# Attention outputs computed transposed, with V stationary in high and low halves

## The reference

```python
s = einsum('bghqd,bgnd->bghqn', qb, kc) * scale
p_cmp = masked_softmax(s, cmp_end <= t)            # cmp: 63 compressed keys
o_cmp = einsum('bghqn,bgnd->bghqd', p_cmp, vc)
...                                                # slc: 16 of 16 blocks of 64 keys are taken
p = masked_softmax(s, pos <= t)
o_slc = einsum('bghqk,bgqkd->bghqd', p, v_sel)
...                                                # win: the last 512 keys
o_win = einsum('bghqk,bgkd->bghqd', p, vwb)
out = gb[..., 0:1] * o_cmp + gb[..., 1:2] * o_slc + gb[..., 2:3] * o_win
```

## Time and profile before

| | us |
|---|---|
| median of 3 runs | 1504.34 |
| lowest, highest | 1502.41, 1508.38 |
| the profiled execution | 1505.05 |
| its span, first to last instruction | 1503.2 |
| attention, four trips | 342 to 683 |

### The profile page before, as it was taken

The page is one execution under the profiler, slowest core; times in us unless marked ns, Lnnn a source line. Parts: engine busy times, 40 slices in busy tenths (PEclk is TensorE's granted clock), DMA queues, the critical chain, the costliest instruction groups (busy, mean ns, idle before and its releaser), DMA issues.

```text
span 1503.2 us, 23026 instructions
## 1 busy us (share of the span) xinstructions
PE 1443.0 (96%) x7958; PEld 1234.4 (82%) x7958; DVE 874.7 (58%) x1633; ACT 627.6 (42%) x1242; POOL 162.3 (11%) x179
## 2 busy tenths in 40 slices
PE   7999999998989899998999998999999999999999
PEld 6888888877878888888997886888888788888887
DVE  2002682106657475668876486666666588668764
ACT  5113302224544445453241256765555654444441
POOL 2433333520000000000033000000000000000000
PEclk9999999999989899899999999999999999999999
DMA  5211114200000000003010014544444865643332
GB/s 165 64 49 49 46 33 125 70 7 2 1 1 0 1 0 1 0 0 134 22 55 31 29 36 142 167 154 153 148 150 152 285 240 168 225 140 99 98 113 84
DMA packets 78248, 129.25 MB, mean 86 GB/s; under 512 B 8973, under 2 KB 26826, under 8 KB 78154
## 3 DMA queue, kind: packets, MB, share of 16 engines
q1 hardware_dynamic: 77968, 128.01, 26.9%
q10 hardware_dynamic: 186, 0.08, 0.0%
HBM read 94.51 MB, written 33.55 MB: 85 GB/s over the span
## 4 chain that ended last, share of the span: by engine, by line
PE 88%; DVE 7%; ACT 2%; issue 2%; DMA 1%; DVEq 0%; ACTq 0%
PE ps L516 62%; PE ps L2120 7%; PE ps L2080 4%; PE ps L2095 4%; PE ps L2143 3%; PE ps L2114 1%; PE ps L1949 1%; PE ps L2085 1%; PE ps L1921 1%; PE ps L2064 1%; PE ps L755 1%; DVE hgrn_A L1618 1%; DVE hgrn_vg L1652 0%; DVE hgrn_k L1609 0%; PE ps L2188 0%
## 5 line engine op out<-in xcount | busy, mean ns | idle before, releaser
L516 PE MATMUL ps<-mlp_w_high,hidden_high 128*128 128x512 f32 x448 | 174.3, 389 | 0.0
L516 PE MATMUL ps<-mlp_w_low,hidden_high 128*128 128x512 f32 x448 | 174.3, 389 | 0.0
L516 PE MATMUL ps<-mlp_w_high,hidden_low 128*128 128x512 f32 x448 | 174.3, 389 | 0.0
L516 PE MATMUL ps<-w_high,hT_high 128*128 128x512 f32 (+1 forms) x448 | 170.5, 380 | 1.6 <-DVE hT_low L1373 0.9
L516 PE MATMUL ps<-w_low,hT_high 128*128 128x512 f32 (+1 forms) x448 | 168.1, 375 | 0.0
L516 PE MATMUL ps<-w_high,hT_low 128*128 128x512 f32 (+1 forms) x448 | 168.0, 375 | 0.0
L2120 PE MATMUL ps<-nsa,probs_T 128*128 x1056 | 139.1, 276 | 0.0
L1683 DVE TENSOR_TENSOR mlp_w_low<-mlp_w_raw,mlp_w_high 128x512 fp32r<-128x512 f32 x112 | 77.1, 691 | 98.3 <-ACT mlp_w_high L1209 98.3
L1308 ACT ACTIVATE mlp_w_high<-mlp_w_raw 128x512 fp32r<-128x512 f32 x112 | 70.6, 630 | 148.3 <-PE ps L516 148.3
L2120 PEld LDWEIGHTS ps<-nsa,probs_T 128*128 128x128 f32 x1056 | 130.5, 195 | 0.0
L1763 DVE TENSOR_TENSOR mlp_w_low<-mlp_w_raw,mlp_w_high 128x512 fp32r<-128x512 f32 x112 | 77.2, 689 | 65.8 <-ACT mlp_w_high L1308 65.8
(11 more groups left out here) (232 smaller groups left out, 2922.1 us busy)
## 6 DMA issues: line engine op xcount, KB each, us to landing
hidden_raw<-hidden_pieces SPq DMA_DIRECT2D x112, 256.0 KB, 2.7
mlp_w_raw<-in_w_mlp_in_dram SPq DMA_DIRECT2D x32, 512.0 KB, 4.4
hidden_pieces<-hidden SPq DMA_DIRECT2D x64, 256.0 KB, 2.7
mlp_w_raw<-in_w_mlp_out_dram SPq DMA_DIRECT2D x64, 256.0 KB, 4.6
w_raw<-in_w_in_dram SPq DMA_DIRECT2D x56, 256.0 KB, 2.7
hidden_pieces<-hidden_s SPq DMA_DIRECT2D x48, 256.0 KB, 2.2
x_in<-in_x_dram SPq DMA_DIRECT2D x8, 512.0 KB, 6.8
w_raw<-in_w_out_dram SPq DMA_DIRECT2D x16, 256.0 KB, 2.6
```

The source lines that it names most:

```text
L516: ins = nc.tensor.matmul(out_ap, a_hl[i], b_hl[j], start=first and n == 0, stop=last and n == 2, skip_group_check=onto_a_sum_already_read)
```

## The change

V of the slc and win branches is split before the loop into a high half (fp32r) and the rest, and laid out as 64 high and 64 low columns for each kind and group (v_split, in nsa). The transposed probabilities of two token tiles t-1 and t lie side by side as 256 columns, in a high and a low half (PT, two sets): ScalarE copies every group out of its PSUM bank as the high half, then VectorE subtracts for the low half, and both must be done before TensorE writes the bank again. For each pair of token tiles TensorE holds a V block of 128 columns and streams the 256 high and then the 256 low columns (outputs_T): rows 0 to 63 of the result are from V's high half, 64 to 127 from its low one. slc and win fill one bank together. ScalarE copies the bank (oT), TensorE transposes it back in four blocks (outputs_back) into the seventh bank, ScalarE copies that to o_rows, and GpSimd adds the halves, multiplies by the coefficients and adds both branches onto nsa, four operations a pair (rows_pool). VectorE forms the coefficients once for a pair. The cmp items stay as they were, with ScalarE making their copy.

The new buffers take hv's place: SP stores hv to DRAM (hv_kept) as its quarters are ready, the last two after the masks, and loads it again after the last rows of attention (y_done), ahead of w_out; ScalarE, GpSimd and TensorE wait for the stores (TensorE through the memsets of the unused blocks, zeroed). TensorE's loop over g and both of GpSimd's loops are written out. The HGRN2 stage now begins with the last transposes back (oT_back). The w2 loads of four chunks share one semaphore and the hidden loads use x_loaded.

```diff
@@ -297,7 +291,15 @@
     KS_L = sb("k_low", [P, 2, NG, S], F32R, 16384)
     QT = sb("q_stack", [P, 2, S], F32R, 32768)
     probs = sb("probs", [P, P_SLOTS, S], F32, 65536)
-    pT = sb("probs_T", [P, PT_SLOTS, BW], F32, 40960)
+    W2T = 2 * P
+    PT = [{"slc": [sb(f"probs_T_slc{n}_{s}", [P, ns, W2T], F32R, a) for s, a in zip(("high", "low"), at2)],
+           "win": [sb(f"probs_T_win{n}_{s}", [P, 6, W2T], F32R, a) for s, a in zip(("high", "low"), at3)]}
+          for n, ns, at2, at3 in ((0, 6, (HV_AT, HV_AT + 6144), (HV_AT + 12288, HV_AT + 18432)),
+                                  (1, 8, (40960, 49152), (83968, HV_AT + 24576)))]
+    cmp_pT = sb("cmp_probs_T", [P, BW], F32, 59392)
+    oT = sb("outputs_T", [P, BW], F32, 57344)
+    o_rows = sb("outputs_high_low", [P, 4, 2, DK], F32, HV_AT + 30720)
+    v_split = sb("v_high_low", [P, NT, NSAW], F32R, NSA_AT)
     masks = sb("masks", [P, 3 * P], BF16, 61440)
     cmask = sb("cmask", [P, NT * NCP], BF16, 62464)
     cdiff = sb("cmp_diff", [P, BW], F32, 81920)
...
-        n = it.groups[m]["ptn"] - PT_SLOTS
-        if n >= 0:
-            old = [u for u in it.groups if u.get("ptn") == n][0]
-            eng.wait_ge(pv_done, ib + (old["item"] + 1))
+    def pt_slots(j, m):
+        kind, hh, t, tiles = it.items[j]
+        u = it.groups[m]
+        r = 1 - t % 2 + u["first"]
+        cols = slice(t % 2 * P, (t % 2 + 1) * P)
+        return [x[:, r:r + u["n"], cols] for x in PT[t // 2 % 2][kind]]
+    def by_head(c0, part):
+        return v_split[:, :, c0:c0 + 4 * DK].rearrange("p t (g a d) -> p t g a d", g=NG, a=2)[:, :, :, part, :]
+    def v_rows(c0):
+        return nsa[:, :, c0:c0 + 2 * DK].rearrange("p t (g d) -> p t g d", g=NG)
+    V_AT = {"slc": KC0, "win": KS0}
+    hv_kept = nc.dram_tensor("hgrn_v_and_gate", (P, 2, NT, HH * P), F32, kind="Internal").ap()
     def flat(ap):
...
                         load_chunk(sp, n, j, w_in0[j * P:(j + 1) * P, bass.ds(i * BW + col0, BW)])
+            def store_hv(i, half):
+                sp.wait_ge(proj_out, 40 + 8 * i + 4 * half + 4)
+                sp.dma_start(hv_kept[:, i, 4 * half:4 * half + 4, :], hv[:, i, 4 * half:4 * half + 4, :]).then_inc(hv_stored, 16)
+            for half in range(2):
+                store_hv(0, half)
             sp.wait_ge(w_used, W_OUT_AT)
...
+            for half in range(2):
+                store_hv(1, half)
+            sp.wait_ge(oT_back, 4 * NPT)
             sp.dma_start(tree[:, :, :].rearrange("p n t -> p (n t)"), c_tree).then_inc(t_loaded, 16)
+            sp.wait_ge(y_done, 4 * NPT + 1)
+            for i in range(2):
+                sp.dma_start(hv[:, i, :, :], hv_kept[:, i, :, :]).then_inc(hv_loaded[i], 16)
             for m in range(16):
                 if m == RING:
                     sp.wait_ge(q_up, 2)
...
+            pool.wait_ge(hv_stored, 64)
+            for n in range(2):
+                for kind, r, c0 in (("slc", 0, 0), ("win", 0, 0), ("win", 5, P)):
+                    for x in PT[n][kind]:
+                        pool.memset(x[:, r, c0:c0 + P].bitcast(F32), 0.0).then_inc(zeroed, 1)
+            pool.sem_inc(y_done)
+            ys = Steps(y_step)
+            def rows_pool(g, pr, n):
+                trip = g * 2 + pr
+                hh, t = n // 4, 2 * (n % 4)
+                u = o_rows[:, :, 0, :]
+                u4 = u.rearrange("p (b t) d -> p b t d", b=2)
+                y = nsa[:, t:t + 2, bass.ds(g * 256 + pr * 128 + hh * DK, DK)]
+                c = coef[:, hh, t:t + 2, :].rearrange("p t b -> p b t").unsqueeze(3).to_broadcast([P, 2, 2, DK])
+                pool.wait_ge(o_out, trip * NPT + (n + 2))
+                ys.mark(pool.tensor_tensor(u, u, o_rows[:, :, 1, :], ALU.add))
+                pool.wait_ge(coef_ready, trip * NPT + (n + 1))
+                ys.wait(pool)
+                ys.mark(pool.tensor_tensor(u4, u4, c, ALU.mult))
+                ys.wait(pool)
+                pool.wait_ge(cmp_y, trip * 2 + (hh + 1))
+                ys.mark(pool.tensor_tensor(y, u4[:, 0, :, :], y, ALU.add))
+                ys.wait(pool)
+                pool.tensor_tensor(y, u4[:, 1, :, :], y, ALU.add).then_inc(y_done, 1)
+            for g in range(NG):
+                for pr in range(2):
                     trip = g * 2 + pr
                     pool.wait_ge(t_full, trip * len(it.groups) + FIRST)
                     stand_alone(pool)
                     stage_head(None, 1, nsa[:, :, bass.ds(g * 256 + pr * 128 + DK, DK)])
-                    stage_head(None, 0, nsa[:, :, bass.ds(g * 256 + pr * 128 + 2 * DK, DK)])
+                    col = (trip + 1) * 2 * DK if trip < 3 else KW0
+                    stage_head(None, 0, nsa[:, :, col:col + DK])
+                    for n in range(NPT):
+                        rows_pool(g, pr, n)
             pool.wait_ge(f_up, 14)
...
                 act.wait_ge(t_full, 8 + half + 1)
                 act.activation(QT[:, 0, half * BW:(half + 1) * BW], ps[:, key_bank(8 + half), :], ACT.Copy).then_inc(t_act, 1)
+            act.activation(by_head(KC0, 0), v_rows(VS0), ACT.Copy).then_inc(v_high, 1)
+            act.wait_ge(v_low, 1)
+            act.wait_ge(stage_ready, 4)
+            act.activation(by_head(KS0, 0), v_rows(VW0), ACT.Copy).then_inc(v_high, 1)
+            act.sem_inc(o_out)
             def out_act(act, c):
                 act.wait_ge(O_full, c + 1)
...
+                def outputs_T_act(i, n):
+                    act.wait_ge(pv_done, i * NPT + (n + 1))
+                    if n:
+                        act.wait_ge(oT_back, i * NPT + n)
+                    act.activation(oT[:], ps[:, O_BANK, :], ACT.Copy).then_inc(oT_out, 1)
+                def output_rows_act(i, n):
+                    act.wait_ge(oT_back, i * NPT + (n + 1))
+                    act.wait_ge(y_done, i * NPT + (n + 1))
+                    act.activation(o_rows[:].rearrange("p i a d -> p (i a d)"), ps[:, B_BANK, :], ACT.Copy).then_inc(o_out, 1)
                 table_for(act, ACT.Exp)
                 exponentials(0)
...
+                        act.wait_ge(t_full, tb + (m + 1))
+                        n = it.pair_of(j)
+                        if kind == "cmp":
+                            if hh:
+                                act.wait_ge(cmp_pv_done, i * 2 + 1)
+                            act.activation(cmp_pT[:], ps[:, T_BANK + m % 2, :], ACT.Copy).then_inc(t_act, 1)
+                            continue
+                        if n >= 2:
...
+                            .then_inc(t_act, 1)
                     if j + 2 < len(it.items):
                         exponentials(j + 2)
+                    if it.second(j - 1) and it.items[j - 1][0] == "win":
+                        outputs_T_act(i, it.pair_of(j - 1))
+                    if it.second(j - 2) and it.items[j - 2][0] == "win":
+                        output_rows_act(i, it.pair_of(j - 2))
+                outputs_T_act(i, NPT - 1)
+                output_rows_act(i, NPT - 1)
+            act.wait_ge(hv_stored, 64)
             with act.Fori(0, NG) as g:
...
+            for n, (kind, c0) in enumerate((("slc", VS0), ("win", VW0))):
+                dve.wait_ge(v_high, n + 1)
+                dve.tensor_tensor(by_head(V_AT[kind], 1), v_rows(c0), by_head(V_AT[kind], 0).bitcast(F32), ALU.subtract).then_inc(v_low, 1)
...
-                    at_.mark(dve.reciprocal(c, rsums[:, hh, t, :]))
+                    at_.mark(dve.reciprocal(c, rsums[:, hh, t - 1:t + 1, :]))
                     at_.wait(dve)
-                    at_.mark(dve.tensor_tensor(c, c, gates[:, t, bass.ds(head3 + 1, 2)], ALU.mult))
-                    at_.wait(dve)
-                    dve.wait_ge(pv_done, ib + (j + 1))
-                    dve.wait_ge(o_free, i * 18 + (hh * 9 + 1))
-                    o_bank = O_BANK + it.pair(j) % 2
...
+                        high, low = pt_slots(j, m)
+                        dve.wait_ge(t_act, ab + u["act_after"])
+                        dve.tensor_tensor(low, ps[:, T_BANK + m % 2, 0:u["n"] * P].rearrange("p (n t) -> p n t", t=P),
+                                          high.bitcast(F32), ALU.subtract).then_inc(t_dve, 1)
+                    if kind == "win" and it.second(j):
+                        coefficients(j)
+                    if j >= 2 and it.items[j - 2][0] == "cmp":
+                        cmp_rows(j - 2)
             with dve.Fori(0, NG) as g:
                 with dve.Fori(0, 2) as pr:
...
                             pe.wait_ge(exp_done, ib + (u + 1))
                         if it.items[u][0] == "cmp":
-                            pe.wait_ge(o_free, i * 18 + (it.items[u][1] * 9 + 1))
+                            pe.wait_ge(cmp_y, i * 2 + (it.items[u][1] + 1))
                     if kind == "cmp":
                         pe.wait_ge(t_dve, vb + (it.groups[it.prep[1][1]]["dve_after"] if hh else 0))
...
                 def transposes(j):
                     pe.wait_ge(exp_done, ib + (j + 1))
```

(51 more changed lines are left out.)

167 lines of the change are left out of this document (72 added, 95 removed).

## The result

The changed kernel takes 1520.86 us (median; 1519.32 to 1525.32) against 1505.39 of the kernel before beside it: ratio 1.011, 95% interval 1.0084 to 1.0135. It is slower by some 16 us. I had said 1497, faster or the same, with 1514 as the upper end: both side and range were wrong.

The account below looks back on a forecast made before the run. TensorE, busy 79.2 of 85.7 us a trip, was taken to set the pace; -32.4 + 21 + 3.6 - 2.4 + 1.0 = -9.2 us, gain rounded down by 1, took 1505 to 1497, with 8 in 10 for 1478 to 1514.

Parts of the forecast that it names:

- Removed work: TensorE's output products in attention: old ones out, new ones and transposes back in, -46.8 + 14.4 = -32.4 us over four trips.
- Work taken from TensorE counts in full: Attention trips: TensorE sets the pace, so its savings count whole while the transposes, ScalarE, VectorE chain stays shorter.
- The bank round: Transposing banks passing through ScalarE, then VectorE: 2.13 us a round, waits of 5.2 us a trip, 21 in four (0 to 40).
- No engine's sum reaches TensorE's 70: Attention trips: VectorE near 56 us, ScalarE 61, GpSimd 2.3 a pair, all below TensorE's 70.
- rival (b): Attention pairs: ScalarE's copies fall into the bank round, 0.6 us at each of 32 pairs, +19, 1516 us; chance 13%.
- Start: Before attention's first scores: V is split first, in two rounds of about 2.25 us, +3.6 us (bounds +3.5 and +8.5).
- Rival (a): Trip tails: the clock falls, the last two outputs take twice as long, 13 us in four trips, 1510 us; chance 25%.
- (c): Bank round in attention: costs nothing, so without its 21 us the forecast is 1476 us; chance 15%.
- (d): Start of attention: held by the store to DRAM, +5 us on the forecast, 1502 us; chance 5%.
- Boundaries: Between trips: 6.1 us in place of 6.5, VectorE's code arriving under the outputs; -2.4 us in all.
- End: After the last output of attention: copy, way back and rows copy, 3.35 us for 1.85, +1.5, of which +1.0 not yet counted.
- Loads back, w2 waits: After attention: two 2 MB loads ahead of w_out (10 us) hide behind more than 25 us of work; w2's waits add nothing.

Follow-up runs that it names:

- The run with fewer blocks: The kernel before with 28 of the 132 output blocks of each trip left out: 1479.51 us, ratio 0.9833.
- the experiment in which removed work turned to waits: The changed kernel without the products of the probabilities' low halves (76 of 152 output products a trip): 1493.63 us, ratio 0.9921.
- a further bank: The changed kernel with a third bank for transposed probabilities, the transposes back moved into the outputs' own bank: 1514.10 us, ratio 1.0068.
- the two fastest kernels: By median: the kernel before with output blocks left out (1479.51 us); the changed kernel with three edits, stores off the start and transposes back later (1485.94 us).

## Why the prediction was wrong, point by point

- **Removed work: mis-sized, -25.6 in place of -32.4.** The 0.113 between two loads was right for loads of one group (0.112), but I took it for all of them. The step from a group's last load to the transposes behind it is only 0.06, so in the earlier trace rows the ten begin at 542.89 and what follows them at 543.97, and ten elsewhere take 1.07. At 0.107 on the average a block is 0.214, and a trip's 28.2, not 29.6. Added products: 0.12 apart where I had 0.118 (575.26, 575.38, 575.50, 575.62; in longer groups 0.117 to 0.12); transposes back 4 in 0.45 as forecast. The run with fewer blocks agrees: 20 blocks less took 4.26 us off, 0.213 each.
- **"Work taken from TensorE counts in full": right for the kernel before** (4.26 of 4.28 to 4.5 us), wrong for the changed one (three quarters). I had tied it to the chain of transposes, ScalarE and VectorE staying shorter than TensorE's work, and in the changed kernel it does not stay so everywhere.
- **The bank round: the wait was there, at the size and the places given** (4.6 us a trip for 5.2). On the old products it costs 10.5 to 11.8 us (21 forecast). In the changed kernel more, some 17 by what the other terms leave; that fits the experiment in which removed work turned to waits, but no run isolates it.
- **The step that failed: the added work of VectorE and ScalarE was taken to hide because of their sums ("the others have 32 us or more to spare", "No engine's sum reaches TensorE's 70"), and only the round "with both engines free" was charged.** The sums were right (54 to 56 and 54 to 58 us a trip for 56 and 61; GpSimd 0.73 + 0.61 + 0.46 + 0.46 = 2.3 us a pair, as said), but the order in the queues was not looked at, and stood in the sum at nothing but 0.3 us a trip. The compressed rows behind a low half cost 12.4 us (9.8 by the profiled spans without the clock), the rows' copy and the transposes back ahead of an item's copy 8.3 (5.6 in the same way). The second is rival (b) at less than half its price, to which I gave 13%; the first stood in no rival, though the diff shows the row step behind the low halves in VectorE's loop.
- **Start: +3.6 right, the clock left out.** I took the half-clock stretch at each trip's start as unchanged, having put it down to idling just before; a pause three times as long made it 20.5 us. The trace has 13.7 us more of half clock in all: 4.1 us (20 more by the mean clocks of all executions: 6). And such a stretch costs 0.3 of its length here, not the half that I wrote.
- **Rival (a), clock at the tails: false.** The Trainium skill's rule that I weighed there ("TensorE: Matmul & The Clock Gate", Part 4: PE-mode transpose), read as a fall at every tail, is not borne out. From 597.84 to 602.60 TensorE had nothing but transposes, with waits between them, and the clock was 1.00 in that stretch and behind it. **(c), the round costs nothing: false. (d): not in this kernel.**
- **Boundaries: the 2.4 us of gain did not come.** From the last output load to the next trip's first transposes it is 6.4, 6.6 and 6.3 us, where I had 6.1, and before it was 6.4, 6.4 and 6.1. VectorE's late start is gone, as I said; ScalarE's table load took its place. **End: nearly as forecast**, 3.25 us for 2.08 (+1.2 for +1.5). **Loads back, w2 waits: nothing seen**; all behind attention adds 0.3.

The sum as it came out, in us of the profiled span: work -25.6, start +3.6, clock +4.1, compressed rows +9.8, copies around the transposes back +5.6, all else inside the trips +17.6 (by difference: bank round, boundaries and end, for which I had 21 - 2.4 + 1.0 = 19.6), behind attention +0.3: +15.4. The rows and copies are from the profiled spans of the runs less 0.3 for each us of half clock that went (all executions give 9.7 and 6.2), the clock from 0.3 a us, and the first term from the loads' spacing. Against my -9.2 it is 24.6 us more: 15.4 from the order in the queues, 6.8 from the work, 4.1 from the clock, 0.3 from behind attention, less 2.0 for the bank round, boundaries and end.

In the one stretch where all is at full clock the waits can be read directly: low halves 3.8, compressed rows 1.9, outputs' copy 1.3 and exponentials 0.9, against 0.8 of such before: 7.1 more, less 4.5 of work, is about the 2.5 us that it grew.

**Open:** why the second, third and fourth trips have 3.4 us of half clock in one trace and 13.7 in another. It moves a trace by up to 3 us a trip. It is no fixed property of a kernel, since executions of one kernel differ in their mean clock, and nothing that I read forecasts it.

## What to carry to other kernels

When a change lets each buffer pass through two engines in turn, don't add up busy time: write out each engine's queue around one item, and look for an instruction that waits for something recent in front of one that somebody needs now. Moving two such instructions without changing any work was worth 12.4 and 8.3 us here (some 10 and 6 without the clock that went with them), more than a further bank. And price a longer pause of TensorE by what the clock does after it, not only by its length.

## What the hardware showed

- The pause of TensorE ahead of attention and the half clock (1.2 GHz) of the first trip behind it, each in one execution: 6.6 us and 17 to 20.5 (six kernels), 3.7 us and 13.6 (two), 2.1 us and 6.8 (three) or nothing (the two fastest kernels). With unused products in the pause there was none. A us at half clock cost 0.3 us of this attention (0.29 by the 44 executions of the kernel before); that much of it waits on other engines would explain it, but no run isolates that.
- TensorE with transposes alone for 4.8 us (22 loads, 2.2 us of loading) kept its full clock.
- fp32r products of 256 columns start 0.12 us apart, float32 ones of 64 columns 0.112 for each of their two passes, so the first kind streams four times the columns in about the time of one pass of the second.
- The half clock of a trip's start differs from trip to trip of one execution though all do the same work (13.7, 3.4 and 13.7 us behind the first in the changed kernel), and the mean clock from execution to execution of one kernel (0.977 to 0.987 before).
